# Heads of the even attention squared, rooted and normed beside the last two products of their projection; decay sums and decays moved in between attention units; the odd output projection begun inside the odd attention

## The chip, the cores and the metric

The kernel runs on one core of one Trainium2 chip. The metric is the device time of one execution in microseconds (us), as the median of several runs.

## The reference

Two blocks of a transformer with two mixers each, in fp32, on 256 context and 256 latent tokens (T = 512) of width 1024. In the first block each mixer is followed by a feed-forward part. The even mixer of the first block is what most of the change concerns:

```
def qkv_a(p, T):
    q, k, v = jnp.split(p[..., :A_COLS], A_SPLITS, axis=-1)
    q = rms_norm(q.reshape(Bsz, T, A_HEADS, HEAD_DIM), q_gain)
    k = rms_norm(k.reshape(Bsz, T, A_KV_HEADS, HEAD_DIM), k_gain)
    return q, k, v.reshape(Bsz, T, A_KV_HEADS, HEAD_DIM)
...
oa_lat, oa_ctx = global_gqa(apply_rope(q_l, cos, sin), apply_rope(k_l, cos, sin), v_l, q_c, k_c, v_c, ctx_out)
f_lat = rwkv7_features(p_lat[..., A_COLS:], mu, w0, w2, a0, a2, g2, k_k, k_a)
...
o_lat = jnp.concatenate([oa_lat, ob_lat], axis=-1) @ w_out
```

The odd mixer projects q, k and v, rotates q and k, attends within a window plus the context with a sink column in the softmax, and multiplies the result by w_out.

## The kernel before, in words

The program is written engine by engine, with semaphores between the engines; each engine runs its list in order. A projection takes its weights in slabs of 128 output channels (512 KB each, a ring of four slots that SyncE fills). Each slab is split into a high part (ScalarE, split_hi, L403) and a low part (VectorE, split_lo, L408; for a stage's first slabs GpSimd, as gpsimd_splits says), and TensorE makes three matmuls per tile of 128 input channels (L502 to L504), 8 tiles to a product. High and low parts of slab m lie in place m % 2, so slab m + 2 can be split only when product m is done. The number of a product within its stage is m.

**Even stage.** linear_tensor(0) makes 21 products (m = 0 to 20). Products 0 to 14 feed the recurrent (rwkv) branch, 15 to 18 are four tiles of q heads, 19 is k, 20 is v. Beside each step linear_scalar and linear_vector advance the generators wkv_ahead_scalar and wkv_ahead_vector by one yield; linear_tensor calls wkv_ahead_tensor(r) behind each run r of LINEAR_RUNS. Behind product 18 (r = 2) it makes the low-rank products of units 0 and 1 (L2049, L2050), whose sigmoids (wkv_rates_scalar, L2212, L2213) ScalarE takes behind products 19 and 20. Then even_heads_* run: ScalarE squares five tiles (L1538), TensorE sums them over each head (L1557), ScalarE takes the logarithm (L1541) and the exponential (L1545), VectorE norms (L1572), TensorE turns (L1563), VectorE multiplies by cosine and sine (L1517, L1520) and adds (L1524). VectorE first makes the decay sums of units 0 and 1 (wkv_decay_sums, a scan L2362 and a subtraction L2364), and ScalarE at the end their decays (wkv_decays_scalar, L2221 to L2223). heads_ready then lets attend_tensor(0) start.

**Attention.** attend_tensor, attend_vector and attend_scalar go over units (head pair, query tile), 16 of them: scores (L1379), the rows' maximum (L1429), exponentials (L1490), reciprocal and scaling (L1452, L1456), transposes (L1388), their copy (L1499), the mix with v (L1402) and its copy out. They are staggered: iteration it makes the scores of unit it, the transposes of unit it - 2 and the mix of unit it - 3. GpSimd has keys, factors and rho of units 0 and 1 (L2306 to L2327) to make for the recurrence that follows the attention; the factors wait for the decays.

**Odd stage.** linear_tensor(1) makes 12 products with the attention woven in between; the attention's last iterations run alone. odd_beside_scalar splits the high parts of slabs 0 and 1 of the output projection behind iteration 13, GpSimd their low parts. residual_tensor(1) then makes 8 products on the 256 latent columns, behind the whole attention; residual_vector makes the low parts of the eight tiles of attention output (L1149) and of slabs 2 to 7. GpSimd's next instruction behind its two low parts is the DMA of the second block's context.

## Time and profile before

| | us |
|---|---|
| median of 3 runs | 2657.34 (2656.98 to 2659.55) |
| the profiled execution | 2659.08 |
| its span | 2657.3 |
| TensorE busy | 2479.8 (93%) |
| VectorE busy | 1697.6 (64%) |
| ScalarE busy | 1061.6 (40%) |
| GpSimd busy | 424.8 (16%) |

The span goes from the first to the last instruction of the profiled execution. Busy shares are averages over stages with different limits; the chain of work that ended last tells which engine the end waited for, and an engine's timeline tells, in brackets, how long it stood idle before an instruction and what ended that.

### The profile page before, as it was taken

The numbers are of one execution on the slowest core, as the hardware profiler recorded it, in microseconds if no ns is written. First come the engines' busy times: TensorE is split into PE (matmuls) and PEld (weight loads), VectorE is DVE, ScalarE is ACT, GpSimd is POOL, SyncE is SP. The second block draws the span as 40 slices with busy tenths as digits, with TensorE's granted clock in tenths as the row PEclk, the third lists the DMA queues.
The fourth block names the chain that finished last, engine by engine and source line by source line (L and its number), as shares of the span: only waits on it lengthen the run. The fifth ranks groups of instructions, "written<-read, shape, count | busy, mean of one in ns | idle before, by whom it ended". The sixth has DMA issues, their size and how long they took to land.

```text
span 2657.3 us, 49498 instructions
## 1 busy us (share of the span) xinstructions
PE 2479.8 (93%) x19578; PEld 2030.9 (76%) x19578; DVE 1697.6 (64%) x2785; ACT 1061.6 (40%) x1750; POOL 424.8 (16%) x374
## 2 busy tenths in 40 slices
PE   6999999969888999999999999879999998889977
PEld 4888888737777778888888888659997874577856
DVE  2877887565454687778787763675555325565664
ACT  4222224354423552222522223555455243545344
POOL 2000001023445410000100001001012700111042
PEclk9999999989999999999999999999999999999999
DMA  7766662200000256666466653215563231013401
GB/s 259 227 195 191 195 205 93 84 5 3 4 3 5 65 175 193 193 194 203 150 212 190 193 161 97 76 57 163 182 176 117 88 91 48 1 64 119 126 18 48
DMA packets 88434, 323.55 MB, mean 122 GB/s; under 512 B 9712, under 2 KB 10864, under 8 KB 87504
## 3 DMA queue, kind: packets, MB, share of 16 engines
q1 hardware_dynamic: 86864, 310.68, 38.5%
q0 software_dynamic: 1408, 10.59, 1.1%
q8 instruction: 117, 1.92, 0.3%
q14 instruction: 45, 0.37, 0.0%
HBM read 320.18 MB, written 1.05 MB: 121 GB/s over the span
## 4 chain that ended last, share of the span: by engine, by line
PE 79%; DVE 9%; ACT 5%; issue 4%; DVEq 1%; DMA 1%; POOL 0%; POOLq 0%; ACTq 0%; SPq 0%
PE bank L502 21%; PE bank L504 21%; PE bank L503 21%; PE bank L2126 4%; PE bank L1388 1%; PE bank L1379 1%; DMA weight_ring<-stream_k 1%; DVE row_statistics L1429 1%; DVE weights_hi_lo L408 1%; ACT work L1490 1%; PE bank L1402 1%; ACT work L1499 1%; ACT weights_hi_lo L403 1%; PE bank L1771 1%; PE bank L2749 1%
## 5 line engine op out<-in xcount | busy, mean ns | idle before, releaser
L403 ACT ACTIVATE weights_hi_lo<-weight_ring 128x1024 fp32r<-128x1024 f32 (+1 forms) x381 | 397.3, 1043 | 1082.5 <-PE bank L504 1058.0
L408 DVE TENSOR_TENSOR weights_hi_lo<-weight_ring,weights_hi_lo 128x1024 fp32r<-128x1024 f32 (+1 forms) x372 | 452.3, 1216 | 481.8 <-ACT weights_hi_lo L403 480.2
L502 PE MATMUL bank<-input_hi,weights_hi_lo 128*128 128x512 f32 (+1 forms) x2032 | 742.5, 365 | 18.7 <-DVE input_lo L813 11.9
L503 PE MATMUL bank<-input_lo,weights_hi_lo 128*128 128x512 f32 (+1 forms) x2032 | 739.3, 364 | 0.0
L504 PE MATMUL bank<-input_hi,weights_hi_lo 128*128 128x512 f32 (+1 forms) x2032 | 739.0, 364 | 0.0
L502 PEld LDWEIGHTS bank<-input_hi,weights_hi_lo 128*128 128x128 f32 x2032 | 385.5, 190 | 85.5 <-issue 22.8
L503 PEld LDWEIGHTS bank<-input_lo,weights_hi_lo 128*128 128x128 f32 x2032 | 385.7, 190 | 59.9 <-issue 0.5
L504 PEld LDWEIGHTS bank<-input_hi,weights_hi_lo 128*128 128x128 f32 x2032 | 385.5, 190 | 60.1
L502 PE MATMUL bank<-hidden_hi_lo,weights_hi_lo 128*128 128x512 f32 (+1 forms) x952 | 342.0, 359 | 4.0 <-DVE hidden_hi_lo L1113 2.1
L503 PE MATMUL bank<-hidden_hi_lo,weights_hi_lo 128*128 128x512 f32 (+1 forms) x952 | 339.0, 356 | 0.0
L504 PE MATMUL bank<-hidden_hi_lo,weights_hi_lo 128*128 128x512 f32 (+1 forms) x952 | 339.0, 356 | 0.0
L754 POOL TENSOR_TENSOR work<-work 128x512 f32<-128x512 f32 (+1 forms) x48 | 70.6, 1471 | 1135.7 <-ACT work L642 1134.6
L552 DVE CUSTOM_DVE_ANT_0 work<-weight_ring,extra_tiles 128x1024 f32<-128x1024 f32 x176 | 224.6, 1276 | 36.0 <-issue 13.3
L553 DVE CUSTOM_DVE_ANT_0 weight_ring<-weight_ring,extra_tiles 128x1024 f32<-128x1024 f32 x176 | 214.9, 1221 | 0.0
L502 PEld LDWEIGHTS bank<-hidden_hi_lo,weights_hi_lo 128*128 128x128 f32 x952 | 179.8, 189 | 33.6 <-DVE hidden_hi_lo L1113 4.0
L503 PEld LDWEIGHTS bank<-hidden_hi_lo,weights_hi_lo 128*128 128x128 f32 x952 | 179.9, 189 | 26.1 <-issue 0.7
L504 PEld LDWEIGHTS bank<-hidden_hi_lo,weights_hi_lo 128*128 128x128 f32 x952 | 179.9, 189 | 25.7
L1278 DVE TENSOR_TENSOR work<-work,bank 128x512 f32<-128x512 f32 (+1 forms) x88 | 54.7, 622 | 52.9 <-PE bank L504 45.4
L1429 DVE TENSOR_REDUCE row_statistics<-bank 128x2 f32<-128x1024 f32 (+2 forms) x56 | 55.8, 996 | 42.2 <-PE bank L1379 40.4
L1490 ACT ACTIVATE work<-bank,row_statistics 128x512 f32<-128x512 f32 (+1 forms) x80 | 47.5, 598 | 67.9 <-DVE row_statistics L1429 48.2
L2272 POOL TENSOR_TENSOR work<-work,constants 128x512 f32<-128x512 f32 x40 | 52.0, 1307 | 120.4 <-DVE work L2372 68.3
L1388 PEld LDWEIGHTS bank<-constants,work 128*128 128x128 f32 x256 | 29.3, 147 | 50.6 <-issue 47.8
(514 smaller groups left out, 3116.6 us busy)
## 6 DMA issues: line engine op xcount, KB each, us to landing
weight_ring<-stream_k SPq DMA_DIRECT2D x498, 512.0 KB, 3.8
weight_ring<-stream_f SPq DMA_DIRECT2D x64, 448.0 KB, 3.5
weight_ring<-stream_f SPq DMA_DIRECT2D x32, 512.0 KB, 3.7
extra_tiles<-condrows POOLq DMA_DIRECT2D x3, 1024.0 KB, 8.6
constants<-consts POOLq DMA_DIRECT2D x1, 2112.5 KB, 9.1
residual_stream<-xin SPq DMA_DIRECT2D x1, 2048.0 KB, 12.3
work<-nabias POOLq DMA_DIRECT2D x1, 2048.0 KB, 9.4
residual_stream<-ctx POOLq DMA_DIRECT2D x1, 1024.0 KB, 7.9
```

The source lines that it names most:

```text
L403: act.activation(split_place(place)[:, 0, 0:words], w[:, 0:words], ACT.Copy).then_inc(hi_ready, 1)
L408: eng.tensor_tensor(split_place(place)[:, 1, 0:words], ring[:, n % RING, 0:words], split_place(place)[:, 0, 0:words].bitcast(F32), ALU.sub ...
L502: pe.matmul(out, weights[:, 0, w], x_hi, start=first, stop=False)
L503: pe.matmul(out, weights[:, 0, w], x_lo, start=False, stop=False)
L504: return pe.matmul(out, weights[:, 1, w], x_hi, start=False, stop=last)
L552: dve.tensor_tensor_reduce(PRODUCTS, w, COND[:, 0, :], 1.0, 0.0, ALU.mult, ALU.add, MOD_SUMS[:, j, 0:1])
L553: dve.tensor_tensor_reduce(w, w, COND[:, 1, :], 1.0, 0.0, ALU.mult, ALU.add, MOD_SUMS[:, j, 1:2]) .then_inc(mod_read, 1)
L754: pool.tensor_tensor(total, total, squares_of(place, kt)[:, a:b], ALU.add)
L1388: mm = pe.transpose(pb[4 + b][:, tok(i)], attention_probs(which, u)[:, b, tok(i)], C("ident"))
L1429: ins = dve.tensor_reduce(st[:, 0, :], sc[:, :, 0:nk], AX.X, ALU.max, negate=True)
L1490: ins = act.activation(attention_probs(which, it)[:, b, 0:nk], pb[2 * (it % 2) + b][:, 0:nk], ACT.Exp, bias=st[:, 0, b:b + 1], accum_out=s ...
L2126: mm = pe.matmul(pb[bank][half, o], x[half, o], y[half, o], start=True, stop=True)
```

## The change

**Even projection.** The last run of LINEAR_RUNS is cut in two. ScalarE squares tiles 0 to 3 behind product 18, takes both pairs of sigmoids there and loads its table; behind product 19 it squares tile 4 and takes the roots of tiles 0 to 3, one after another. TensorE sums tiles 0 to 3 between products 19 and 20, in banks 4 to 7. VectorE norms tiles 0 to 3 and makes their cosine products behind product 19. What is left of even_heads_* is the root, norm and rotation of tile 4, the turns, sine products and adds, and the transposes of v. **Decays.** VectorE makes the decay sums behind iterations 2 and 5 of the even attention, ScalarE the decays behind iterations 4 and 7. **Odd output.** gpsimd_splits is 0 for it: VectorE makes the low parts of slabs 0 and 1 behind the attention's last scaling. ScalarE splits their high parts behind iterations 14 and 15 instead of both behind 13. TensorE makes 6 of 8 tiles of product 0 before the last unit's mix and 7 of 8 tiles of product 1 behind it, and the rest in odd_out_rest.

In the diff the removed lines of even_heads_scalar, even_heads_tensor, even_heads_vector, residual_tensor and residual_vector are left out; they stand in the kernel above.

```diff
-return 0 if stage.startswith("ffn_out") else 2 if stage.endswith("_out") else 1
+return 0 if stage.startswith("ffn_out") or stage == "odd_out" else 2 if stage.endswith("_out") else 1
...
-LINEAR_RUNS = [[(13, ALL), (3, ALL), (3, ALL), (2, ALL)], [(4, ALL), (8, LAT)], [(30, ALL)], [(1, ALL), (4, ALL), (4, ALL), (4, LAT), (8, ALL), (8, LAT)]]
+LINEAR_RUNS = [[(13, ALL), (3, ALL), (3, ALL), (1, ALL), (1, ALL)], [(4, ALL), (8, LAT)], [(30, ALL)], [(1, ALL), (4, ALL), (4, ALL), (4, LAT), (8, ALL), (8, LAT)]]
...
-    OUT_SLOTS = {0: (range(KT), range(KT, 2 * KT)), 2: ((38, 39, 41, 5, 6, 7, 8, 10), (13, 14, 15, 16, 0, 1, 2, 3)),
+    OUT_SLOTS = {0: (range(KT), range(KT, 2 * KT)), 1: (range(28, 36), range(36, 44)), 2: ((38, 39, 41, 5, 6, 7, 8, 10), (13, 14, 15, 16, 0, 1, 2, 3)),
...
-            if n >= 4 and m < 2:
+            if m < 2 and (n >= 4 or r == 1):
...
+    def odd_out_half(pe, m, kts):
+        pe.wait_ge(split_ready, VECTOR_SPLIT_AT["odd_out"][0] + m + 1)
+        half_products(pe, 1, m, kts)
+    def odd_out_rest(pe):
+        half_products(pe, 1, 0, range(6, KT))
+        half_products(pe, 1, 1, range(KT - 1, KT))
+        for m in range(2, KT):
+            pe.wait_ge(split_ready, VECTOR_SPLIT_AT["odd_out"][0] + m + 1)
+            pe.wait_ge(mixer_added, KT + m + 1)
+            half_products(pe, 1, m, range(KT))
...
+    def odd_tile_lo(dve, kt):
+        dve.wait_ge(mixer_hi, KT + kt + 1)
+        dve.tensor_tensor(out_lo(1, kt), BIG[:, kt, TC:T], out_hi(1, kt).bitcast(F32), ALU.subtract).then_inc(mixer_split, 1)
+        if r == 1:
+            split_lo(dve, 0, n0, s0 + 1)
+            for kt in range(6):
+                odd_tile_lo(dve, kt)
+            split_lo(dve, 1, n0 + 1, s0 + 2)
+            for kt in range(6, KT):
+                odd_tile_lo(dve, kt)
...
     def attend_tensor(pe, a):
...
+                if which == "odd" and u == n - 1:
+                    odd_out_half(pe, 0, range(6))
                 pe.wait_ge(turned_copied, u0 + u + 1)
                 mm.then_inc(mixed, 1)
+                if which == "odd" and u == n - 1:
+                    odd_out_half(pe, 1, range(KT - 1))
...
+    EVEN_BANKS = (4, 5, 6, 7, 1)
+    EVEN_TILES = [WORK[:, 15 + i, :] for i in range(5)]
+    def even_square(act, i):
+        act.wait_ge(*linear_copied(0, 15 + i))
+        act.activation(EVEN_TILES[i], BIG[:, EVEN_Q + i, :], ACT.Square).then_inc(qk_squared, 1)
+    def even_root(act, i):
+        act.wait_ge(qk_summed, i + 1)
+        act.activation(EVEN_TILES[i], pb[EVEN_BANKS[i]][:, :], ACT.Ln, bias=epsb[:, 1:2] if i < 4 else epsb[:, 0:1],
+                       scale=1.0 if i < 4 else 1.0 / HD)
+        act.drain()
+        act.activation(pb[EVEN_BANKS[i]][:, :], EVEN_TILES[i], ACT.Exp, scale=-0.5).then_inc(qk_rooted, 1)
     def even_heads_scalar(act):
+        even_root(act, 4)
         act.wait_ge(values_turned, 1)
+        act.activation(BIG[:, 28, :], pb[2][:, :], ACT.Copy).then_inc(values_ready, 1)
+    def even_sum(pe, i):
+        pe.wait_ge(qk_squared, i + 1)
+        pe.matmul(pb[EVEN_BANKS[i]][:, :], C("blk"), EVEN_TILES[i], start=True, stop=True).then_inc(qk_summed, 1)
+    def even_turn(pe, i):
+        pe.wait_ge(qk_normed, i + 1)
+        pe.matmul(pb[EVEN_BANKS[i]][:, TC:T], C("rot"), BIG[:, EVEN_Q + i, TC:T], start=True, stop=True)\
+          .then_inc(qk_turned, 1)
     def even_heads_tensor(pe):
+        even_sum(pe, 4)
+        for i in range(4):
+            even_turn(pe, i)
+        pe.wait_ge(*linear_copied(0, 20))
         for tt in range(TT):
+            mm = pe.transpose(pb[2][:, tt * P:(tt + 1) * P], BIG[:, EVEN_Q + 5, tt * P:(tt + 1) * P], C("ident"))
         mm.then_inc(values_turned, 1)
+        even_turn(pe, 4)
+    def even_norm(dve, i):
+        q = BIG[:, EVEN_Q + i, :]
+        dve.wait_ge(qk_rooted, i + 1)
+        dve.scalar_tensor_tensor(out=q, in0=q, scalar=V("qgain" if i < 4 else "kgain"), in1=pb[EVEN_BANKS[i]][:, :],
+                                 op0=ALU.mult, op1=ALU.mult).then_inc(qk_normed, 1)
+    def even_cosine(dve, i):
+        dve.tensor_tensor(EVEN_TILES[i][:, 0:TC], BIG[:, EVEN_Q + i, TC:T], C("cosa"), ALU.mult)
+    def even_sine(dve, i):
+        dve.wait_ge(qk_turned, i + 1)
+        dve.tensor_tensor(EVEN_TILES[i][:, TC:T], pb[EVEN_BANKS[i]][:, TC:T], C("sina"), ALU.mult)
+    def even_rotated(dve, i):
+        return dve.tensor_tensor(BIG[:, EVEN_Q + i, TC:T], EVEN_TILES[i][:, 0:TC], EVEN_TILES[i][:, TC:T], ALU.add)
     def even_heads_vector(dve):
+        for i in range(4):
+            even_sine(dve, i)
+        dve.drain()
+        for i in range(4):
+            even_rotated(dve, i)
+        even_norm(dve, 4)
+        dve.drain()
+        even_cosine(dve, 4)
+        even_sine(dve, 4)
+        dve.drain()
+        even_rotated(dve, 4)
+        dve.drain().then_inc(heads_ready, 1)
         dve.wait_ge(tables_loaded, 16)
...
     def odd_beside_scalar(act):
...
             yield
         next(attention)
         for k in range(2):
+            next(attention)
             first_split_scalar(act, "odd_out", k)
         yield from attention
         act.drain().then_inc(mixer_ready, KT)
...
     def wkv_ahead_vector(dve):
...
         dve.drain().then_inc(kk_ready, 1)
         yield
+        yield
+        for i in range(4):
+            even_norm(dve, i)
+        dve.drain()
+        for i in range(4):
+            even_cosine(dve, i)
+        yield
...
     def wkv_ahead_scalar(act):
...
         act.activation(BIG[:, GL, :], BIG[:, GL, :], ACT.Sigmoid).then_inc(ranks_ready, 1)
         yield
         yield
+        for i in range(4):
+            even_square(act, i)
+        for n in range(2):
+            wkv_rates_scalar(act, n)
+        act.preload_act_table_set(LN_EXP)
         yield
-        wkv_rates_scalar(act, 0)
+        even_square(act, 4)
+        for i in range(4):
+            even_root(act, i)
         yield
-        wkv_rates_scalar(act, 1)
-        act.preload_act_table_set(LN_EXP)
...
     def wkv_ahead_tensor(pe, r):
...
+        if r == 3:
+            pe.wait_ge(rates_ready, 2)
+            for i in range(4):
+                even_sum(pe, i)
...
-        residual_tensor(pe, 1)
+        odd_out_rest(pe)
...
         norm_vector(dve, 1, "even_in")
         linear_vector(dve, 0, wkv_ahead_vector(dve))
         even_heads_vector(dve)
-        for _ in attend_vector(dve, 0):
-            pass
+        for it, _ in enumerate(attend_vector(dve, 0)):
+            if it in (2, 5):
+                wkv_decay_sums(dve, it // 3)
         wkv_vector(dve)
...
-        for _ in attend_scalar(act, 0):
-            pass
+        for it, _ in enumerate(attend_scalar(act, 0)):
+            if it in (4, 7):
+                wkv_decays_scalar(act, it // 7)
```

ScalarE from the low ranks' activations on, at products 17 to 20 (L1020 copies a product, L2212 and L2213 are sigmoids, L1538 squares, L1541 and L1545 the root). Before:

```order
L403 ACTIVATE weights_hi_lo<-weight_ring 128x1024 x2
L1020 ACTIVATE projections<-bank 128x512
L2212 ACTIVATE work<-bank,vectors 128x512
L2213 ACTIVATE work<-bank,vectors 128x512
L1020 ACTIVATE projections<-bank 128x512
L2212 ACTIVATE projections<-bank,vectors 128x512
L2213 ACTIVATE projections<-bank,vectors 128x512
L1945 ACT_TABLE_LOAD
L1538 ACTIVATE work<-projections 128x512 x5
L1541 ACTIVATE work<-bank,epsilons 128x512 x5
L1545 ACTIVATE bank<-work 128x512 x5
```

And now (L2263 and L2264 are the sigmoids, L1545 squares, L1550 and L1553 the root of a tile):

```order
L1020 ACTIVATE projections<-bank 128x512
L1545 ACTIVATE work<-projections 128x512 x4
L2263 ACTIVATE work<-bank,vectors 128x512
L2264 ACTIVATE work<-bank,vectors 128x512
L2263 ACTIVATE projections<-bank,vectors 128x512
L2264 ACTIVATE projections<-bank,vectors 128x512
L1990 ACT_TABLE_LOAD
L1545 ACTIVATE work<-projections 128x512
L1550 ACTIVATE work<-bank,epsilons 128x512
L1553 ACTIVATE bank<-work 128x512
L1550 ACTIVATE work<-bank,epsilons 128x512
L1553 ACTIVATE bank<-work 128x512
```

Four squares and both pairs of sigmoids moved ahead of the last copy, the table load ahead of all that, and the roots are taken tile by tile.

VectorE in the first iterations of the even attention (L1434 maximum, L1457 and L1461 scaling, L2413 and L2415 the decay sum's scan and subtraction). Now:

```order
L1434 TENSOR_REDUCE row_statistics<-bank 128x2
L1457 RECIPROCAL row_statistics<-row_statistics 128x2
L1461 TENSOR_SCALAR work<-work,row_statistics 128x256 x2
L2413 SCALAR_TENSOR_TENSOR work<-spare_tiles,work 128x512
L2415 TENSOR_TENSOR work<-work 128x512
L1434 TENSOR_REDUCE row_statistics<-bank 128x2
L1457 RECIPROCAL row_statistics<-row_statistics 128x2
```

Before, the scan and subtraction of both units stood ahead of the norms of the heads:

```order
L1040 COPY projections<-bank 128x512
L2362 SCALAR_TENSOR_TENSOR work<-spare_tiles,work 128x512
L2364 TENSOR_TENSOR work<-work 128x512
L2362 SCALAR_TENSOR_TENSOR projections<-spare_tiles,projections 128x512
L2364 TENSOR_TENSOR projections<-projections 128x512
L1572 SCALAR_TENSOR_TENSOR projections<-projections,vectors,bank 128x512 x5
```

The decay sums left the heads' path and stand between the scaling behind one maximum and the next maximum; the second one likewise, three iterations later.

VectorE at the end of the odd attention (L1454 and L1461, before L1449 and L1456, scale the last probabilities; L1139, before L1149, makes the low parts of output tiles; L1054 adds a product to the residual). Before:

```order
L1449 SCALAR_TENSOR_TENSOR row_statistics<-row_statistics,constants 128x2
L1452 RECIPROCAL row_statistics<-row_statistics 128x2
L1456 TENSOR_SCALAR projections<-projections,row_statistics 128x384 x2
L1149 TENSOR_TENSOR hidden_hi_lo<-projections,hidden_hi_lo 128x256 x8
L408 TENSOR_TENSOR weights_hi_lo<-weight_ring,weights_hi_lo 128x1024
L1054 SCALAR_TENSOR_TENSOR residual_stream<-bank,modulation,residual_stream 128x256
```

And now:

```order
L1454 SCALAR_TENSOR_TENSOR row_statistics<-row_statistics,constants 128x2
L1457 RECIPROCAL row_statistics<-row_statistics 128x2
L1461 TENSOR_SCALAR projections<-projections,row_statistics 128x384 x2
L408 TENSOR_TENSOR weights_hi_lo<-weight_ring,weights_hi_lo 128x1024
L1139 TENSOR_TENSOR hidden_hi_lo<-projections,hidden_hi_lo 128x256 x6
L408 TENSOR_TENSOR weights_hi_lo<-weight_ring,weights_hi_lo 128x1024
L1139 TENSOR_TENSOR hidden_hi_lo<-projections,hidden_hi_lo 128x256 x2
L408 TENSOR_TENSOR weights_hi_lo<-weight_ring,weights_hi_lo 128x1024
L1054 SCALAR_TENSOR_TENSOR residual_stream<-bank,modulation,residual_stream 128x256
```

Two low parts of weights that GpSimd made are now VectorE's, ahead of the output tiles 0 and 6.

## Rows read from the trace of the kernel before

A timeline's row gives start in us, duration in us, engine, line, operation, out<-in, shapes, and how many instructions are merged (x); in brackets the idle time before it and what ended it. DVE is VectorE, ACT ScalarE, POOL GpSimd, PE TensorE.

**Rows 1.** The page: the chain that ended last, shares of the span by engine.

```profile
PE 79%; DVE 9%; ACT 5%; issue 4%; DVEq 1%; DMA 1%; POOL 0%; POOLq 0%; ACTq 0%; SPq 0%
```

**Rows 2.** Busy time by stretch (us; x is instructions; then TensorE's granted clock, DMA).

```profile
558.00:566.00 8.00, 7.00 (x20) 2.71 (x20) 4.31 (x9) 3.68 (x13) 6.23 (x6) 0.50 0.00 0
566.00:614.00 48.00, 37.42 (x336) 24.63 (x336) 27.91 (x71) 27.40 (x68) 0.00 (x0) 0.96 0.01 1
1764.00:1787.00 23.00, 13.70 (x120) 9.67 (x117) 17.11 (x44) 14.59 (x39) 5.68 (x3) 0.93 0.29 93
```

**Rows 3.** Timeline of TensorE, 480 to 575 us: start, us, what [idle before it].

```profile
482.06 3.59 PE L1952 MATMUL bank<-work,constants 128*128 128x512 f32 x8
...
538.89 6.09 PE L1557 MATMUL bank<-work,constants 128*128 128x512 f32 x10 [3.94 <-ACT work L1538]
...
547.21 4.05 PE L1563 MATMUL bank<-projections,constants 128*128 128x256 f32 x10 [1.79 <-DVE projections L1572]
...
557.80 2.08 PE L1379 MATMUL bank<-projections 64*128 64x256 f32 x8 [6.54 <-DVEq L1577]
```

**Rows 4.** Timeline of ScalarE around the end of the even projection.

```profile
529.55 0.69 ACT L2212 ACTIVATE work<-bank,vectors 128x512 f32<-128x512 f32 x1 [7.90 <-PE bank L504]
...
545.77 2.68 ACT L1545 ACTIVATE bank<-work 128x512 f32<-128x512 f32 x5
...
549.90 0.62 ACT L2223 ACTIVATE work<-work 128x512 f32<-128x512 f32 x1
```

**Rows 5.** Timeline of VectorE, same stretch.

```profile
538.31 1.23 DVE L2362 TENSOR_TENSOR_SCAN work<-spare_tiles,work 128x512 f32<-128x512 f32 x1 [8.07 <-DMA spare_tiles<-tables]
...
542.93 0.69 DVE L2364 TENSOR_TENSOR projections<-projections 128x512 f32<-128x512 f32 x1
...
546.41 3.38 DVE L1572 SCALAR_TENSOR_TENSOR projections<-projections,vectors,bank 128x512 f32<-128x512 f32 x5 [2.78 <-ACT bank L1545]
...
550.56 0.42 DVE L1517 SCALAR_TENSOR_TENSOR work<-projections,constants 128x256 f32<-128x256 f32 x1
...
551.23 1.17 DVE L1517 SCALAR_TENSOR_TENSOR work<-projections,constants 128x256 f32<-128x256 f32 x1
...
555.95 1.77 DVE L1524 TENSOR_TENSOR projections<-work 128x256 f32<-128x256 f32 x5
```

**Rows 6.** Timeline of GpSimd, same stretch.

```profile
550.60 1.51 POOL L2317 TENSOR_TENSOR work<-work,projections 128x512 f32<-128x512 f32 x1 [8.82 <-ACT work L2223]
...
563.10 1.27 POOL L2327 TENSOR_TENSOR work<-projections,extra_tiles 128x512 f32<-128x512 f32 x1
```

**Rows 7.** Timelines in the even attention: VectorE (first two), ScalarE (last).

```profile
566.05 1.23 DVE L1429 TENSOR_REDUCE row_statistics<-bank 128x2 f32<-128x1024 f32 x1 [1.06 <-PE bank L1379]
...
575.83 1.23 DVE L1429 TENSOR_REDUCE row_statistics<-bank 128x2 f32<-128x1024 f32 x1 [2.45 <-PE bank L1379]
...
573.79 0.47 ACT L1490 ACTIVATE work<-bank,row_statistics 128x256 f32<-128x256 f32 x1 [1.31 <-PE bank L1388]
```

**Rows 8.** Timelines at the end of the odd attention: GpSimd, then VectorE.

```profile
1770.62 4.66 POOL L408 TENSOR_TENSOR weights_hi_lo<-weight_ring,weights_hi_lo 128x1024 fp32r<-128x1024 f32 x2 [93.87 <-ACT weights_hi_lo L403]
...
1767.91 0.75 DVE L1456 TENSOR_SCALAR projections<-projections,row_statistics 128x384 f32<-128x384 f32 x2
...
1770.84 2.15 DVE L1449 SCALAR_TENSOR_TENSOR row_statistics<-row_statistics,constants 128x2 f32<-128x2 f32 x1
...
1773.31 2.51 DVE L1456 TENSOR_SCALAR projections<-projections,row_statistics 128x384 f32<-128x384 f32 x2
```

**Rows 9.** The same, TensorE, ScalarE (two), then VectorE.

```profile
1786.23 0.39 PE L502 MATMUL bank<-hidden_hi_lo,weights_hi_lo 128*128 128x256 f32 x1
...
1789.41 1.06 ACT L403 ACTIVATE weights_hi_lo<-weight_ring 128x1024 fp32r<-128x1024 f32 x1 [2.30 <-PE bank L504]
...
1792.29 1.06 ACT L403 ACTIVATE weights_hi_lo<-weight_ring 128x1024 fp32r<-128x1024 f32 x1 [1.82 <-PE bank L504]
...
1790.50 1.23 DVE L408 TENSOR_TENSOR weights_hi_lo<-weight_ring,weights_hi_lo 128x1024 fp32r<-128x1024 f32 x1 [2.93 <-ACT weights_hi_lo L403]
```

59 lines of the change are left out of this document (1 added, 58 removed).

## The prediction

> **What bounds the kernel now.** I read the page first. The chain that ended last is TensorE for 79% of the span, VectorE 9%, ScalarE 5% [rows 1]: wherever matmuls are queued nothing else counts, and time can only be won where TensorE waits. So I next read TensorE's timeline at the two places that the diff touches.
>
> First place, the even projection's end. The last product ends at 534.95 us (538.89 less its idle 3.94), the first score matmul of the even attention starts at 557.80 [rows 3]: 22.85 us, in which the 4 heads of q and k are squared, summed, rooted, normed and rotated stage by stage. TensorE's sums wait for ScalarE's squares until 538.89 [rows 3], VectorE's norms start at 546.41, its last adds at 555.95 [rows 5]. The decay sums and decays stand in the same queues, on VectorE from 538.31 [rows 5], and on ScalarE the first unit's decays end at 550.5 [rows 4]. GpSimd works beside this, and the rows show what it costs: L1517 (two operands in SBUF) takes 0.42 us alone and 1.17 us at 551.23, while GpSimd's 1.51 us operation from 550.60 still runs [rows 5, 6].
>
> Second place, the odd attention's end. At 1770.62 GpSimd computes the low parts of two slabs of the output projection in 4.66 us. In that time VectorE's L1449 on 128x2 takes 2.15 us, ending at 1772.99, about where GpSimd's first of the two ends (1770.62 + 4.66/2), and L1456 takes 2.51 us, against 0.75 us just before [rows 8]. That is some 3.7 us of stall (2.15 less an estimated 0.2 for two columns, and 2.51 less 0.75) on the engine that the softmax waits for. The output products then start at 1786.23, 2.88 us each (the pitch of ScalarE's splits, 1789.41 to 1792.29) [rows 9].
>
> **Term A, until the even attention starts.** Squares and rates of tiles 0 to 3 now follow product 18 on ScalarE. Product 19 ends at 529.55, when ScalarE starts its sigmoids [rows 4], and product 20 takes 5.4 us, so 19 began near 524.1; the two pairs of sigmoids (0.69 us each) and the table load end near 528.5 (before, the 3.94 us up to 538.89 held the copy, one pair, the load and the first square). I take this as hidden. TensorE then does 4 of the 5 sums between the products: 8 matmuls of 512 columns, 3.59 us for 8 at 482.06, of which 3.43 are pitch [rows 3]. So product 20 ends 3.4 us later, at 538.4. Its 5.4 us cover ScalarE's square and roots of tiles 0 to 3 (a logarithm at the sigmoid's 0.69 us, an exponential of 2.68/5 = 0.54, 1.3 us with the drain between, 5.2 together, done near 536.2) and VectorE's norms (3.38/5 = 0.68 each) [rows 4, 5], which end near 537.
>
> After product 20 remain: the fifth sum, 0.9 us; four turns of 256 columns, half a sum each, 1.7; the last sine product, 0.4; four adds, 1.4 (1.77/5 each); the norm of k 0.7; its turn 0.4, sine 0.4, add and drain 0.6 [rows 3, 5]. With 0.3 us for handing over, 6.8 us. GpSimd's keys of unit 1 come here, three operations behind the table load that waits for product 20, and the adds have two operands in SBUF. From below the lock costs nothing; from above 2.6 us, as the adds may be held by two whole GpSimd operations of 1.3 us (1.27 at 563.10) [rows 6]. The nearest row is L1517's, held for 0.75; with two such meetings, 1.3 us. Attention starts at 538.4 + 8.1 = 546.5 instead of 557.8: **-11.3 us**.
>
> **Term B, inside the even attention.** VectorE gets a scan of 1.23 us [rows 5] and a subtraction that I put at the 0.7 of a 512-column norm, 1.9 us with the drain, behind units 2 and 5. Behind unit 2 it idles 1.06 us before the next maximum, behind unit 5 it idles 2.45 us [rows 7]. The first insertion therefore delays every later unit by about 0.9, the second hides unless something else holds it. Queued behind them are the next maxima, for which ScalarE's exponentials and through them TensorE's transposes wait. ScalarE gets three exponentials, 1.6 us, behind units 4 and 7, where it idles 1.31 us [rows 7]: 0.3 us twice, 0.6 or less. GpSimd's two bursts of factors and rho (five operations each; the second ended at 564.37 before [rows 6]) fall behind these exponentials, beside the second decay sum and the scalings of the probabilities. From below 0, from above all of their time, 2 x 5.6 us (four operations of 1.3 and a small one). The nearest row is again L1517, held 0.75 us by one operation: ten would be 7.5, but VectorE idles in most units, and its maxima read PSUM as L1520 does, not two tiles in SBUF. I take a fifth, 1.5. Against it the first two units no longer meet the second burst: -0.5, from one hold of L1517's size. **+2.5 us**.
>
> The Trainium skill, page "SBUF — State Buffer", section "Who interferes with whom", says that a VectorE instruction with two SBUF inputs, or in a two-port mode, and a GpSimd instruction that reads SBUF lock each other out for whole instructions, while tensor_reduce never contends. Both stalls above agree with it. By that rule the maxima are free, but the scan, the subtraction and the scalings can be held; it speaks against moving the decays into the attention, and all of it held would make term B about +12 instead of +2.5.
>
> **Term C, the odd attention's end.** VectorE now makes the two low parts itself, behind its last scaling, and GpSimd does nothing there: up to -3.7 us. Each of ScalarE's two splits now stands one unit later; it costs nothing, or gives 0.3. The clock, 0.93 over 1764 to 1787 us [rows 2], means 3.2 us at half rate there; with shorter gaps I expect -1.2. Together the last transposes come 5.2 us earlier. Six tiles of product 0 (6 x 0.36 = 2.2 us, from 2.88/8 [rows 9]) now stand before the last mix: moved, not removed. After the mix ten tiles remain instead of sixteen. But products 0 and 1 now end 0.4 us apart, and slab 2 goes into slab 0's place: its split starts only when product 0 is done. It takes 2.6 us (ScalarE begins 0.3 behind the product's end at 1789.11, 1.06 and 1.23 us of work [rows 9]), which product 1's 2.88 covered so far. **A new wait** of 2.3 us stands before product 2, with the cover gone. Sum: -5.2 + 2.3, and 0.2 for handing over, **-2.7 us**; between +1 (no tail won, wait full) and -5 (no wait). The context's DMA moves ahead of the odd projection on GpSimd's queue; the projection's weights are four slabs ahead, so I cost it at nothing, and at 1 us without that cover.
>
> **Sum.** -11.3 + 2.5 - 2.7 = -11.5 us. The profiled execution took 2659.08 us for a span of 2657.3; it becomes 2647.6. The median of the runs is 1.7 us lower, 2657.34, so I predict **2645.8 us**. A measurement of this kernel can tell about 0.2%, 5.3 us, from no change.
>
> **Rivals.**
> 1. The attention keeps TensorE's clock up (chance 0.15). Before, it began at the lower level (granted 0.50 for 558 to 566 us) after a stage with long gaps, and rose to 0.96 afterwards [rows 2]. If the shorter gap leaves it at 2.4 GHz, half of the 7.0 us busy there goes, 3 us, and 1 us more elsewhere: -15.5, 2641.8 us. Against it: a gap of 3.94 us was followed by matmuls at half rate, 6.09 us for 10 where 4.3 is the pitch [rows 3], and one of 4 us remains.
> 2. The port eats it (0.12): the bursts hold scans and scalings for most of their length, term B becomes +8 to +9: -5.5, 2651.8 us. For it speaks L1517; against it VectorE's idle time.
> 3. The change doesn't do what it says at product 20 (0.08): rates or squares are late, TensorE waits for them in front of the sums and stands idle with product 20 behind it. Each microsecond late costs one; 3 us late: -8.5, 2648.8 us.
> 4. Slower (0.05): the clock stays at 1.2 GHz through the whole attention. It starts sparse, and the inserted work thins its units 3 to 8. TensorE is busy 37.42 of 48 us at 0.96 [rows 2]; at half rate its work is 75 us, so +27: -11.5 + 27 = +15.5, 2672.8 us. It decides from 11.5/27 = 43% of the attention at the lower level. Against it: after 8 us at 0.50 the clock rose by itself, since a slower TensorE is busy 7.0 of 8 [rows 2].
>
> **Numbers.** My forecast has 0.60. The unknown bounds (A 2.6, B 2 to either side, C 3) rarely add up, so it spans some 2641 to 2650. The range reaches to rivals 1 to 3: **2639.5 to 2652 us**. Faster by over 0.2% holds the forecast, rivals 1 and 3 and half of 2: **0.90**. Within 0.2%: **0.07**. Slower by over 0.2%: **0.03**, most of rival 4.
>
> **What would show it.** Right: TensorE's 8 sum matmuls stand between the last two products without a wait; the first score matmul starts near 546.5; scan and subtraction stand between maxima, with about 1 us more before unit 3's; no GpSimd split near 1770, L1449 back at 0.2 and L1456 at 0.75; the last mix some 3 us earlier; a wait of about 2.3 us in front of product 2 of the odd output. Wrong: TensorE waiting for ScalarE before product 20, more than 12 us of attention at the lower clock, or an attention longer than 60 us (55.8 before).

## The result, and the profile after

The changed kernel takes 2645.61 us (median of 10 runs, 2641.43 to 2656.80) beside 2658.45 us for the kernel before (10 runs, 2655.27 to 2663.84). The ratio is 0.9955 with a 95% interval of 0.9942 to 0.9969: by it the change is 12.0 us faster, between 8.2 and 15.4 (the medians differ by 12.8). The prediction was 2645.8 us. The profiled execution was the slowest of its ten, 2656.80 us with a span of 2655.0, and it is read here beside a second one of the same kernel (the run after_again: 2648.3 us, span 2646.5).

The page of the changed kernel, the chain that ended last by engine (compare [rows 1]):

```profile
PE 80%; DVE 9%; ACT 5%; issue 4%; DVEq 1%; DMA 1%; POOL 0%; POOLq 0%; ACTq 0%; SPq 0%
```

Timeline of TensorE at the end of the even projection, changed kernel (columns as in [rows 3]):

```profile
528.48 3.59 PE L1563 MATMUL bank<-work,constants 128*128 128x512 f32 x8
...
537.37 1.02 PE L1563 MATMUL bank<-work,constants 128*128 128x512 f32 x2
538.23 1.89 PE L1568 MATMUL bank<-projections,constants 128*128 128x256 f32 x8
...
542.80 0.70 PE L1568 MATMUL bank<-projections,constants 128*128 128x256 f32 x2 [2.25 <-DVE projections L1585]
545.17 2.08 PE L1380 MATMUL bank<-projections 64*128 64x256 f32 x8 [1.67 <-DVEq L1613]
```

The eight sum matmuls stand at 528.48 between products 19 and 20 with no idle time before them. Product 20 ends at 537.37, and the first scores follow 7.80 us later, where 22.85 us had passed before [rows 3].

VectorE and ScalarE in the even attention, changed kernel:

```profile
552.34 1.22 DVE L2413 TENSOR_TENSOR_SCAN work<-spare_tiles,work 128x512 f32<-128x512 f32 x1
553.63 0.69 DVE L2415 TENSOR_TENSOR work<-work 128x512 f32<-128x512 f32 x1
554.24 1.22 DVE L1434 TENSOR_REDUCE row_statistics<-bank 128x2 f32<-128x1024 f32 x1
...
563.26 2.26 DVE L2413 TENSOR_TENSOR_SCAN projections<-spare_tiles,projections 128x512 f32<-128x512 f32 x1
565.95 1.19 DVE L2415 TENSOR_TENSOR projections<-projections 128x512 f32<-128x512 f32 x1 [0.43 <-issue]
...
568.42 1.62 DVE L1461 TENSOR_SCALAR work<-work,row_statistics 128x256 f32<-128x256 f32 x2
...
568.31 0.69 ACT L1495 ACTIVATE work<-bank,row_statistics 128x512 f32<-128x512 f32 x1 [3.39 <-DVE row_statistics L1434]
```

And the start of GpSimd's first burst (it ends at 569.9):

```profile
563.17 1.27 POOL L2368 TENSOR_TENSOR work<-work,projections 128x512 f32<-128x512 f32 x1 [19.20 <-ACT work L2274]
```

The first scan and subtraction pass at their own length, and the maximum follows with no idle time, where VectorE had 1.06 us of it before [rows 7]. The second scan meets the burst: 2.26 us where the first takes 1.22, its subtraction 1.19 where 0.69, the scaling at 568.42 1.62 where two such take 0.62 elsewhere. ScalarE's exponentials wait 3.39 us for VectorE's maximum. So in this profile the second insertion was not hidden. With the bursts taken away it is (sums_inside, below).

Timelines at the end of the odd attention, changed kernel: VectorE, then ScalarE, then TensorE (compare [rows 8, 9]):

```profile
1770.12 0.22 DVE L1454 SCALAR_TENSOR_TENSOR row_statistics<-row_statistics,constants 128x2 f32<-128x2 f32 x1
...
1770.65 0.76 DVE L1461 TENSOR_SCALAR projections<-projections,row_statistics 128x384 f32<-128x384 f32 x2
1771.32 1.22 DVE L408 TENSOR_TENSOR weights_hi_lo<-weight_ring,weights_hi_lo 128x1024 fp32r<-128x1024 f32 x1
1772.45 2.10 DVE L1139 TENSOR_TENSOR hidden_hi_lo<-projections,hidden_hi_lo 128x256 fp32r<-128x256 f32 x6
...
1780.89 2.00 ACT L403 ACTIVATE weights_hi_lo<-weight_ring 128x1024 fp32r<-128x1024 f32 x2 [2.65 <-PE bank L504]
...
1783.26 0.48 PE L502 MATMUL bank<-hidden_hi_lo,weights_hi_lo 128*128 128x256 f32 x1 [2.05 <-DVE weights_hi_lo L408]
```

The stall is gone (0.22 and 0.76 us where 2.15 and 2.51 stood [rows 8]), the last mix ends 2.9 us earlier behind the mask of unit 13 (18.1 us where 20.9), and the new wait before product 2 is there: 2.05 us, ended by VectorE's low part of slab 2.

Busy time by stretch, in the columns of [rows 2]; each line runs from marker to marker: low-rank products to first scores; first scores to the even attention's last mix; mask of unit 13 of the odd attention to the last addition (m = 7) of its output projection, the same stretch that the expectations below run to the seventh add; from there to the end. First the kernel before:

```profile
520.18:557.80 37.62, 25.35 (x81) 15.29 (x81) 18.21 (x26) 18.25 (x30) 12.83 (x11) 0.84 0.08 23
557.80:613.56 55.76, 44.58 (x352) 27.50 (x352) 31.93 (x79) 31.08 (x80) 6.41 (x6) 0.90 0.00 1
1765.35:1809.57 44.22, 35.72 (x303) 32.23 (x304) 26.63 (x55) 24.25 (x51) 13.37 (x10) 0.96 0.39 120
1809.57:2657.24 847.67, 782.33 (x4868) 647.00 (x4866) 454.71 (x783) 392.28 (x681) 167.91 (x175) 0.98 0.31 94
```

Then the changed kernel:

```profile
519.31:545.17 25.86, 21.94 (x81) 14.53 (x81) 12.30 (x22) 15.07 (x24) 7.87 (x7) 0.98 0.11 33
545.17:605.49 60.32, 49.14 (x352) 30.23 (x352) 39.02 (x83) 34.04 (x86) 11.75 (x10) 0.81 0.00 1
1759.37:1802.32 42.95, 36.03 (x303) 32.57 (x304) 25.17 (x56) 24.21 (x49) 7.69 (x7) 0.96 0.31 99
1802.32:2654.97 852.65, 789.49 (x4868) 653.32 (x4866) 455.00 (x783) 391.62 (x681) 166.23 (x175) 0.97 0.30 93
```

Stage by stage that is -11.8, +4.6, -1.3 and +5.0 us. With 0.9 us less ahead of the first marker and 2.1 more between the second and the third stage, the span falls by only 2.3 us. The last +5.0 is 4868 matmuls in both, 782.3 us busy in one and 789.5 in the other: the change doesn't touch them, TensorE was longer at its lower level. The even attention too had a granted clock of 0.81 where 0.90 before. The clock has two levels, 1.2 and 2.4 GHz (granted 0.50 and 1.00), so I turn it into time at the lower level as twice the missing share of the stretch: 22.9 us of it against 11.2. Which part of the +4.6 is the clock and which the inserted work is the first thing the experiments had to settle.

### The profile page after: what moved, and what is told of

It is laid out like the page before. It is cut to its first block, busy times and chain, and to the rows that moved or that the text cites. A ratio compares the mean times of both kernels' runs of the same rounds, so it can differ in the third digit from the quotient of the medians.

```text
span 2655.0 us, 49488 instructions
## 1 busy us (share of the span) xinstructions
PE 2489.5 (94%) x19578; PEld 2041.4 (77%) x19578; DVE 1696.8 (64%) x2787; ACT 1059.9 (40%) x1750; POOL 418.4 (16%) x372
## 4 chain that ended last, share of the span: by engine, by line
PE 80%; DVE 9%; ACT 5%; issue 4%; DVEq 1%; DMA 1%; POOL 0%; POOLq 0%; ACTq 0%; SPq 0%
PE bank L502 21%; PE bank L504 21%; PE bank L503 21%; PE bank L2177 4%; PE bank L1389 1%; PE bank L1380 1%; DVE row_statistics L1434 1%; DVE weights_hi_lo L408 1%; PE bank L1405 1%; ACT work L1495 1%; ACT weights_hi_lo L403 1%; DMA weight_ring<-stream_k 1%; PE bank L1809 1%; ACT work L1504 1%; PE bank L2800 1%
## 5 line engine op out<-in xcount | busy, mean ns | idle before, releaser
L502 PEld LDWEIGHTS bank<-input_hi,weights_hi_lo 128*128 128x128 f32 x2032 | 386.6, 190 | 85.7 <-issue 22.9
L1434 DVE TENSOR_REDUCE row_statistics<-bank 128x2 f32<-128x1024 f32 (+2 forms) x56 | 55.7, 995 | 38.8 <-PE bank L1380 36.8
L1389 PEld LDWEIGHTS bank<-constants,work 128*128 128x128 f32 x256 | 32.9, 160 | 51.0 <-issue 43.2
```

Of the source, the lines that this page charges most:

```text
L502: pe.matmul(out, weights[:, 0, w], x_hi, start=first, stop=False)
L1389: mm = pe.transpose(pb[4 + b][:, tok(i)], attention_probs(which, u)[:, b, tok(i)], C("ident"))
L1434: ins = dve.tensor_reduce(st[:, 0, :], sc[:, :, 0:nk], AX.X, ALU.max, negate=True)
```

## The experiments

**The changed kernel again.** No edit.

> The changed kernel once more, for a second profiled execution. Its profile showed the even attention 4.6 us longer than before, with 23.1 us of it at the granted clock's lower level against 11.5, where +2.5 was forecast. If the excess over 2.5 is the clock, a second profile that spends another share of the attention at the lower level differs in the attention's length, by about 1 us per 5 us at the lower level or less, and the engines' durations off TensorE stay. If it is the inserted work, the stage is again 60.7 us whatever the clock. The median should again be 12 us (8 to 15) under that of the kernel before.

Measured: 2648.3 us (7 runs), ratio 0.9953 (0.9936 to 0.9970). The stretch of the even attention:

```profile
541.87:598.21 56.34, 42.98 (x352) 26.46 (x352) 37.10 (x83) 33.97 (x86) 11.10 (x10) 0.93 0.01 1
```

4.0 us shorter with 15 us less at the lower level. Not all of that is the clock. VectorE's busy time fell by 1.9 us as well: the second scan took 1.22 us here, where GpSimd's burst begins only behind its start, and 2.26 in the first profile. From unit 5's maximum to unit 6's pass 4.33 us here and 5.37 there, both at a clock of 1.00. So 1.0 us of the 4.0 is a longer hold, and the other 3.0 are the clock's, which made most of the excess over the forecast.

**Each part alone.** even_only undoes the odd part; odd_only is the kernel before with that part:

```diff
-    return 0 if stage.startswith("ffn_out") or stage == "odd_out" else 2 if stage.endswith("_out") else 1
+    return 0 if stage.startswith("ffn_out") else 2 if stage.endswith("_out") else 1
...
-                    if which == "odd" and u == n - 1:
-                        odd_out_half(pe, 0, range(6))
```

> The change with its odd part undone: GpSimd splits slabs 0 and 1 of the odd output projection, behind iteration 13, and all products stand behind the attention. By the sum of the prediction (terms A -11.3 and B +2.5) it is 8.8 us faster than the kernel before, so about 2649.7, and by the stages measured (-11.8 and +4.6, of which some 2 the clock) 7.2 to 9.5 faster. The stretch from the last but two masks to the odd projection's seventh add has the 44.2 us of the kernel before. Rival (a clock that only shifts): the two parts don't add up, and this kernel alone is as fast as both together, 12 us.

> The kernel before with the odd part of the change alone. Term C of the prediction says 2.7 us faster, the first profile of the changed kernel shows 1.3, or 2.6 without the lower clock that fell on product 2. So 1 to 3 us faster, 2655 to 2657; the stretch from the mask of unit 13 to that of unit 15 falls from 10.4 to 6.9 us, and behind it a wait of 2 to 3 us stands before product 2. Rival (the lock is hidden, product 2 eats everything): within 0.5 us of the kernel before.

Measured: even_only 2648.76 us, ratio 0.9955 (0.9942 to 0.9969); odd_only 2660.83 us, ratio 1.0000 (0.9987 to 1.0012). Both expectations missed: even_only is 11.8 us faster by the medians where I had 7.2 to 9.5, and odd_only is not faster where I had 1 to 3. even_only's stage to the attention has 25.86 us again, its odd stretch 44.20 as before. odd_only's stretch:

```profile
1767.39:1811.90 44.51, 37.60 (x303) 33.81 (x304) 25.11 (x57) 24.22 (x51) 7.71 (x7) 0.92 0.31 96
```

The masks' 10.40 us are 6.93 now, but the stretch as a whole is 0.3 us longer than before at a clock of 0.92. Of the eight profiles with the change's odd part (the two of the change, this one, and those below that leave it alone), three have 42.95 us at 0.96 and five 44.5 us at 0.92; in the five the last mix ends only 1.3 us earlier than before. The even part carries the whole gain that the times show.

**Nothing inserted in the even attention.**

```diff
-                if it in (2, 5):
-                    wkv_decay_sums(dve, it // 3)
+                if it == 19:
+                    for n in range(2):
+                        wkv_decay_sums(dve, n)
```

and ScalarE's decays likewise; sums_inside moves only ScalarE's decays.

> The change with the decay sums and the decays moved behind the even attention's last iteration, so that nothing is inserted in it and GpSimd has nothing to do beside it. If the inserts and GpSimd's bursts cost (term B: 0.9 for the first sum, 0.6 for the exponentials, 1.5 for the bursts), the attention runs 56.5 to 57.7 us at about 12 us of lower clock, 3 to 4 less than the 60.7 measured. If it was the clock alone, the attention has 60 to 61 us again with some 23 us at the lower level. Behind the attention the recurrence then waits for sums, decays and factors: 10 to 14 us are added there, so that the kernel as a whole is 6 to 11 us slower than the changed one. A rival for that: the recurrence's first steps wait for other things and hide half of it, 5 us.

> The change with VectorE's decay sums left behind iterations 2 and 5 of the even attention and ScalarE's decays moved behind its last iteration, so that GpSimd has no burst beside it. Theory: the first sum costs 0.9 us and the rest of the 1.7 us that the inserts cost (57.4 us with them against 55.7 without at 11 us of lower clock) is the exponentials and bursts; the attention up to its last mix is then 56.2 us at about 11 us of lower clock. Rival (the sums alone cost it, the bursts nothing): 57.4. Behind the attention ScalarE's exponentials and GpSimd's factors stand alone, 1.9 and 3.8 us and the handing over, so the recurrence starts 6 us behind the last mix, where 8.2 with the sums behind as well.

Measured: decays_behind 2660.54 us, ratio 0.9997 (0.9985 to 1.0009); sums_inside 2655.07 us, ratio 0.9980 (0.9971 to 0.9989). Their even attention, decays_behind first, then sums_inside:

```profile
544.73:600.02 55.29, 43.84 (x352) 26.98 (x352) 31.58 (x79) 31.08 (x80) 0.00 (x0) 0.91 0.00 1
```

```profile
544.95:600.62 55.67, 43.24 (x352) 26.46 (x352) 35.23 (x83) 32.18 (x83) 0.00 (x0) 0.93 0.00 1
```

The stretches also differ by where the clock was low: at the start, and in before and decays_behind once more near the end, behind unit 15's maximum (9.8 us from there to the last mix, where 8.9 in the others). What the inserts cost is read best from the maxima of units 0 to 15, where decays_behind, sums_inside and after_again have the same pitch except beside an insert. Times from start to start, in us:

| | units 2 to 3 | units 5 to 6 | units 0 to 15 |
|---|---|---|---|
| before | 3.05 | 4.11 | 44.73 |
| decays_behind | 3.05 | 4.11 | 44.72 |
| sums_inside | 3.80 | 4.11 | 45.45 |
| after_again | 3.81 | 4.33 | 46.12 |
| after (first profile) | 3.81 | 5.37 | 50.10 |

The maxima of units 3 and 6, in sums_inside, and of unit 6 in decays_behind:

```profile
554.02 1.22 DVE L1434 TENSOR_REDUCE row_statistics<-bank 128x2 f32<-128x1024 f32 x1
...
563.79 1.22 DVE L1434 TENSOR_REDUCE row_statistics<-bank 128x2 f32<-128x1024 f32 x1 [0.20 <-PE bank L1380]
```

```profile
562.30 1.22 DVE L1434 TENSOR_REDUCE row_statistics<-bank 128x2 f32<-128x1024 f32 x1 [2.45 <-PE bank L1380]
```

Alone, the first sum costs 0.75 us (I had 0.9) and the second nothing: VectorE still waits 0.20 us for the scores behind it. The exponentials and bursts cost 0.7 on top, and all inserts 1.4 us. The first profile's 50.10 is 4.0 us above after_again's, the two kernels being one. There and in even_only the clock fell a second time amid the units, from 26 to 33 and from 13 to 21 us into the attention. It did so in none of before, odd_only, decays_behind and sums_inside, where GpSimd has no burst at that place; whether the inserts bring the fall about, two profiles don't show.

Behind the attention the recurrence of decays_behind waits 8.2 us (4.7 in sums_inside, where I expected 6):

```profile
608.21 1.99 PE L2112 MATMUL bank<-work 64*64 64x64 f32 x64 [8.19 <-POOL work L2372]
```

and takes 5.7 us more itself (272.9 us against 267.2 in after_again, from its first matmul to that of the readout). Of these, 3.2 us fall in its first 25, where GpSimd still makes unit 1's factors ahead of its masks and TensorE runs its first matmuls at the lower level; the other 2.5 were not traced. In all 12.2 us by the medians measured together: I had expected 6 to 11. Once the decays are out of the heads, having them inside the attention and not behind it is thus worth as much as the whole change.

**GpSimd's keys of unit 1 out of the heads.**

```diff
-            wkv_keys(pool, 1)
             for n in range(2):
+                if n:
+                    wkv_keys(pool, 1)
                 wkv_factors(pool, n)
```

> The change with GpSimd's keys of unit 1 moved behind rho of unit 0, so that nothing runs on GpSimd between product 20 and the even attention. The prediction put 1.3 us of the 8.1 us behind product 20 down to these keys (the shared port holds VectorE's products and adds up). If that is so, the stage from the low-rank products to the attention falls from 25.86 to 24.5 us; the port rival at its bound gives 23.3; if the lock costs nothing there, 25.9. In the attention the keys run a little later and lengthen GpSimd's second burst by 3.9 us: at most 1 us more there. As a whole within 2 us of the changed kernel.

Measured: 25.75 us to the attention, where 25.86 to 25.88; the attention 56.36 us at 0.93, as in after_again; 2650.97 us, ratio 0.9970 (0.9958 to 0.9982). The hold by GpSimd's keys costs 0.1 us there, though an instruction takes 1.0 us longer for it. VectorE in the changed kernel, then in keys_later:

```profile
542.83 1.42 DVE L1590 TENSOR_TENSOR work<-projections,constants 128x256 f32<-128x256 f32 x1
544.17 0.41 DVE L1595 TENSOR_TENSOR work<-bank,constants 128x256 f32<-128x256 f32 x1
```

```profile
542.49 0.42 DVE L1590 TENSOR_TENSOR work<-projections,constants 128x256 f32<-128x256 f32 x1
543.72 0.42 DVE L1595 TENSOR_TENSOR work<-bank,constants 128x256 f32<-128x256 f32 x1 [0.80 <-PE bank L1568]
```

Without the keys beside it the cosine product takes 0.42 us, and then VectorE idles 0.80 us for the turn. The hold lay beside a wait. But in keys_later, as in after_again, this turn ran at the lower level (1.22 us for its two matmuls, 0.70 in the first profile). I estimate from the 0.52 us between them that the wait would be some 0.3 us at the upper level, and the hold would cost 0.6; no run has that turn without the keys.

**The norm of tile 4 ahead of the adds.**

```diff
                 even_sine(dve, i)
+            even_norm(dve, 4)
             dve.drain()
             for i in range(4):
                 even_rotated(dve, i)
-            even_norm(dve, 4)
-            dve.drain()
             even_cosine(dve, 4)
```

> The change with VectorE's norm of tile 4 (k) moved ahead of the four adds of tiles 0 to 3. The trace of the change shows TensorE idle for 2.24 us before the turn of tile 4, ended by that norm, and the adds of tiles 0 to 3 (1.43 us) stand ahead of it. If VectorE's row of work is what is left behind product 20, the turn starts 1.4 us earlier and the attention 0.6 to 0.9 us earlier (25.0 to 25.3 us behind the low-rank products, where 25.88). Rival (ScalarE's root of tile 4 is late): no more than 0.2 us. The whole is then within a us of the changed kernel, less than a measurement tells.

Measured: 26.12 us to the attention, 0.25 longer, where I had expected 0.6 to 0.9 less; 2648.92 us, ratio 0.9961 (0.9947 to 0.9975). VectorE, GpSimd and TensorE there:

```profile
541.58 0.74 DVE L1585 SCALAR_TENSOR_TENSOR projections<-projections,vectors,bank 128x512 f32<-128x512 f32 x1
542.41 2.86 DVE L1599 TENSOR_TENSOR projections<-work 128x256 f32<-128x256 f32 x4
...
542.14 0.76 POOL L2358 TENSOR_SCALAR projections<-projections,vectors,one_minus_ka 128x512 f32<-128x512 f32 x1 [1.30 <-issue]
543.05 1.26 POOL L2360 TENSOR_TENSOR projections<-projections 128x512 f32<-128x512 f32 x1
...
546.52 1.34 PE L1380 MATMUL bank<-projections 64*128 64x256 f32 x8 [3.45 <-DVEq L1612]
```

The turn did start early, but the four adds, 1.43 us in the change, now stand beside GpSimd's keys and take 2.86. Neither theory had that: the order of the change puts a wait where the hold falls, mine put work there. This edit with the keys moved away was not run.

**TensorE kept busy ahead of the attention.**

```diff
             mm.then_inc(values_turned, 1)
+            for _ in range(2):
+                pe.matmul(pb[3][:, :], C("blk"), cst[:, 0:T], start=True, stop=True)
             even_turn(pe, 4)
+            for _ in range(2):
+                pe.matmul(pb[3][:, :], C("blk"), cst[:, 0:T], start=True, stop=True)
```

> The change with two full fp32 products of 128 x 512 added on TensorE before the turn of tile 4 and two more behind it, their results unused, so that TensorE stands idle less between product 20 and the first scores. If the lower clock in the even attention comes from that idle time, the attention runs with under 5 us at the lower level and is 1.5 to 4 us shorter (55 to 56 us up to its last mix), the heads 0 to 1.5 us longer because the added products stand in front of the turn and the scores. If the clock follows from what the attention itself does, the attention keeps 8 to 23 us at the lower level and its 56.3 to 60.3 us, and the kernel is 1 us slower.

Measured: 2648.3 us (6 runs), ratio 0.9958 (0.9944 to 0.9972). Up to the attention, and in it:

```profile
517.99:543.86 25.87, 25.35 (x88) 15.93 (x88) 12.31 (x22) 15.07 (x24) 7.94 (x7) 1.00 0.11 33
543.86:598.74 54.88, 39.94 (x353) 25.27 (x352) 37.00 (x83) 33.98 (x86) 11.09 (x10) 1.00 0.01 1
```

The added products cost nothing, and the whole attention ran at the upper level: 54.88 us, 1.5 under after_again. No other kernel but the one that repeats this (best) had more than 0.94 there. That is one profile of each kernel, which makes chance unlikely but doesn't rule it out, and the 1.5 us is less than the runs' medians can tell.

**The odd output: slab 2 in a place of its own; whole products; GpSimd's splits.** slab2_own:

```diff
             for m in range(2, KT):
-                act.wait_ge(slab_done, p0 + m - 1)
-                split_hi(act, m, n0 + m)
+                if r != 1 or m > 2:
+                    act.wait_ge(slab_done, p0 + m - 1)
+                split_hi(act, FIRST if r == 1 and m == 2 else m, n0 + m)
```

The product and VectorE's low part of slab 2 go to that place likewise.

> The change with slab 2 of the odd output projection split into a place of its own, so that its split no longer waits for product 0. The wait before product 2 (2.05 us) goes; if the lower clock that fell on product 2 in each of these kernels came from it, 1.3 us go with it: the stretch from the mask of unit 13 to the seventh add is 39.6 us instead of 42.95, or 40.9 if the clock falls all the same. Rival: product 3 or 4 now waits for its slab (places or the ring), and at most 1 us is gained. As a whole 2 to 3.4 us faster than the changed kernel, 2643 to 2645 beside a kernel before of 2658.

no_halves takes the two calls out of attend_tensor, and pool_splits gives GpSimd the low parts (gpsimd_splits is 2 again, VectorE's two are gone):

```diff
-            half_products(pe, 1, 0, range(6, KT))
-            half_products(pe, 1, 1, range(KT - 1, KT))
+            for m in range(2):
+                odd_out_half(pe, m, range(KT))
```

```diff
-            pe.wait_ge(split_ready, VECTOR_SPLIT_AT["odd_out"][0] + m + 1)
+            pe.wait_ge(first_ready, FIRST_AT["odd_out"][0] + m + 1)
```

> The change with products 0 and 1 of the odd output projection entirely behind the attention, VectorE still making the low parts. The prediction costed the moved tiles at nothing, since TensorE works on them either way and the attention's last mix stands 2.1 us later for them. Then the last mix ends 2.1 us earlier, the first product starts that much earlier, and the stretch to the seventh add is within 0.5 us of the change's 42.95 us (44.4 where the lower clock falls on the last units). Rival (the halves fill a wait of TensorE for the last unit's copies): 1 to 2 us longer.

> The change with GpSimd making the low parts of slabs 0 and 1 of the odd output projection again, behind the mask of unit 13, the rest of the odd part kept. If the shared port is what the kernel before lost there (3.7 us in the prediction, 3.5 measured between the masks of units 13 and 15), that stretch goes back from 6.9 to 10.4 us. Since slabs 0 and 1 then have places of their own, the 2.05 us wait before product 2 and the lower clock on it go too (3.3 us together, 3.7 where slab 2 was given its own place), so that the stretch from the mask of unit 13 to the seventh add is 42.7 to 43.2 us, as good as the change's 42.95. Rival (the masks' stretch was long for another reason): it stays at 6.9 us, and the whole stretch is 39.6.

Measured: slab2_own 2645.90 us, ratio 0.9949 (0.9936 to 0.9963); no_halves 2646.65, 0.9953 (0.9932 to 0.9975); pool_splits 2651.83, 0.9978 (0.9966 to 0.9991). For each kernel the stretch to the last addition; for no_halves, and ahead of it for the changed kernel, also the stretch from the first to the third addition. The changed kernel:

```profile
1783.12:1790.16 7.04, 6.90 (x45) 6.90 (x46) 3.15 (x6) 1.78 (x3) 0.79 (x1) 0.76 0.49 149
```

no_halves:

```profile
1751.18:1792.21 41.03, 35.69 (x303) 32.03 (x304) 25.25 (x57) 24.23 (x51) 7.71 (x7) 0.96 0.32 104
...
1774.28:1780.04 5.76, 5.76 (x51) 5.76 (x50) 3.24 (x5) 2.73 (x4) 0.78 (x1) 1.00 0.51 174
```

slab2_own, then pool_splits:

```profile
1753.65:1794.38 40.73, 35.87 (x303) 32.20 (x304) 25.34 (x56) 24.22 (x49) 7.70 (x7) 0.96 0.34 105
```

```profile
1754.84:1802.45 47.61, 38.81 (x303) 34.74 (x304) 27.20 (x54) 24.29 (x50) 13.30 (x10) 0.89 0.35 112
```

At the same clock of 0.96 the stretch is 44.22 us before, 42.95 in the change, 41.03 without the halves, 40.73 with the halves and a place for slab 2. The halves lose 1.9 us: they take away the cover for slab 2's split, and in the change the clock falls behind the wait (0.76 over the two products), which it does in neither of the other two. I had costed them at nothing in my expectation; that was a miss. With its own place slab 2 brings the halves to 0.3 us better than none. The clock's place differs here too: slab2_own's last units ran at 0.87, as in the five profiles of 44.5 us, and against those its place is worth 3.8 us, and leaving the halves out 3.5. By the medians neither kernel can be told from the change, where I had expected 2 to 3.4 us of slab2_own.

pool_splits missed as well: 47.61 us, where I had expected 42.7 to 43.2. The masks stayed at 6.93 us, because the low parts follow ScalarE's high parts, which the change puts one and two units later; the hold moved there. VectorE, then GpSimd:

```profile
1763.30 2.32 DVE L1433 SCALAR_TENSOR_TENSOR row_statistics<-vectors,row_statistics 128x2 f32<-128x2 f32 x1
...
1768.94 4.26 DVE L1139 TENSOR_TENSOR hidden_hi_lo<-projections,hidden_hi_lo 128x256 fp32r<-128x256 f32 x6
...
1763.26 2.33 POOL L408 TENSOR_TENSOR weights_hi_lo<-weight_ring,weights_hi_lo 128x1024 fp32r<-128x1024 f32 x1 [97.33 <-ACT weights_hi_lo L403]
1769.18 2.39 POOL L408 TENSOR_TENSOR weights_hi_lo<-weight_ring,weights_hi_lo 128x1024 fp32r<-128x1024 f32 x1 [3.58 <-ACT weights_hi_lo L403]
```

A statistics instruction on 2 columns lasts as long as GpSimd's whole instruction, and the six tiles take 4.26 us where 2.10. The wait before product 2 stayed too (2.05 us), since ScalarE's split of slab 2 is written behind product 0 whatever place it goes to. So GpSimd's low parts hold VectorE in the odd tail wherever they stand, and taking them off GpSimd is what gained the 3.5 us between the masks.

**Together.** slab2_own, one added product before the turn of tile 4 and two behind it, and the norm ahead of the adds.

> The change with three edits together: slab 2 of the odd output projection in its own place (3.7 us measured in its stretch), three added products on TensorE ahead of the even attention (the run with four had none of the attention at the lower clock and 54.9 us for it, where 56.3 to 60.3), and the norm of tile 4 ahead of the adds (0.6 to 0.9 us expected). If the added products were the reason for the clock, the attention is again at 54.9 us with at most 3.4 us at the lower level; if that was one draw among the clock's, it has 8 to 23 us of it. Together 5 to 7 us under the changed kernel: 2639 to 2642 beside a kernel before of 2658.6, a ratio of 0.9925 to 0.994.

Measured: 2645.66 us (6 runs, 2638.32 to 2648.87), ratio 0.9955 (0.9939 to 0.9971). Up to the attention, and in it:

```profile
518.27:544.46 26.19, 24.39 (x86) 15.56 (x87) 12.71 (x22) 15.07 (x24) 7.53 (x7) 1.00 0.11 32
544.46:599.31 54.85, 39.93 (x352) 25.25 (x352) 37.32 (x83) 33.93 (x86) 11.09 (x10) 1.00 0.01 1
```

The clock stayed up again, and the odd stretch has 40.73 us again. The three stages sum to 121.8 us against 125.2 in after_again, 3.4 us less, but the ratio is the change's own, where I had expected 5 to 7 us under the change. No kernel here is measurably faster than the change.

## Why the prediction was right

The forecast was right in total and in mechanism; three of its terms were mis-sized, and their errors are of both signs. That it came within 0.2 us of the median is luck: the same kernel had a median of 2648.3 us when measured again, its runs span 15 us, and the terms are off by 0.5 to 3 us each.

**Term A** (-11.3): measured -11.8 in the profile, and the stage had 25.75 to 25.88 us in each of the ten profiles that kept the heads' order. Its two halves came out otherwise. Behind product 20 it took 7.80 us (8.1 in the prediction). Of that I had given 1.3 us to the hold by GpSimd's keys; keys_later shows 0.1 with the turn at the lower level. And I had given 6.8 to the work, which is 7.7: from the turn of tile 4 at 542.46 to VectorE's sine product at 543.72 in keys_later pass 1.26 us, where the prediction had 0.4 and a share of 0.3 for handing over; some 0.5 of it is the turn's lower level.

**Term B** (+2.5): 4.6 us in the first profile, 0.6 in the second, and 1.4 for the inserts by the maxima's pitch. Of the 4.6, 1.4 were the inserts, 1.0 a hold that the second profile doesn't have, and the rest the clock. "The first insertion therefore delays every later unit by about 0.9, the second hides unless something else holds it" came out: 0.75 and nothing in sums_inside, and beside the burst the second took 0.2 us in one profile of the change and 1.3 in the other. The mis-sized part is the exponentials and bursts: 2.1 us less 0.5 in the prediction, 0.7 measured. The 0.5 taken off for the first two units was nothing either, since before and decays_behind agree to 0.01 us over units 0 to 15, with a burst beside the first units in one and none in the other. The two signs named as speaking against me, more than 12 us of attention at the lower clock and an attention over 60 us, both appeared in the first profile. In the second they were gone (7.9 and 56.3 us). They were signs of one execution's clock, and a poor test of the theory.

By the Trainium skill ("SBUF — State Buffer", "Who interferes with whom") the scan, subtraction and scalings can be held and the maxima not. The trace agrees: the maximum between them at 567.06 took its usual 1.21 us while the rest took 1.19 to 2.26. But the +12 us that the prediction gave for a term held whole did not come, and the runs show 1.4.

```profile
567.06 1.21 DVE L1434 TENSOR_REDUCE row_statistics<-bank 128x2 f32<-128x1024 f32 x1
```

**Term C** (-2.7): -1.3 in both profiles of the change, +0.3 in the five where the clock fell once more, and nothing by odd_only's median. The new wait was foreseen with its reason and size (2.3 us, measured 2.05). The stall's removal gave 3.5 us between the masks (3.7 foreseen). The step that failed is "with shorter gaps I expect -1.2" for the clock: it stayed at 0.96 over the stretch in the change, because it now fell on product 2 behind the wait, and in five profiles on the last units too.

**Rivals.** TensorE didn't wait ahead of the sums (rival 3). The clock didn't stay up (rival 1): 0.81 to 0.94 over the attention; in warm and best, with TensorE kept busy ahead of it, it did. The port didn't eat it (rival 2: 1.4 us and not 8 to 9), and the lower level never held a whole attention: 38% of it in the worst profile, under the 43% from which rival 4 decides.
